# A two-layer hybrid attention and expert step: expert rows added in DRAM to the residual stream

## The reference

```
h   = rms_norm(x) * (1 + sc1) + sh1
q, k, v, gates = h @ w_in               # two attention groups, two branch gates
mixed = (sigmoid(g_a) * (o_a @ w_br_a) + sigmoid(g_b) * (o_b @ w_br_b)) @ w_out
x   = x + gt1 * mixed
h2  = rms_norm(x) * (1 + sc2) + sh2
x   = x + gt2 * moe(h2)                 # 16 experts, each token goes to 2 of them
```

## Time and profile before

| what | value |
|---|---|
| runs shown | 1655.37, 1662.59, 1666.16 us |
| median | 1662.59 us |
| span of the profiled execution | 1665.8 us |
| clock granted to TensorE, mean | 0.974 of full speed |
| PE busy | 1550.5 us, 93% of the span |
| DVE busy | 899.4 us, 54% |
| ACT busy | 700.1 us, 42% |
| POOL busy | 297.8 us, 18% |
| moved by DMA | 337.55 MB |

### The profile page before, as it was taken

The page is one execution under the profiler, slowest core; times in us unless marked ns, Lnnn a source line. Parts: engine busy times, 40 slices in busy tenths (PEclk is TensorE's granted clock), DMA queues, the critical chain, the costliest instruction groups (busy, mean ns, idle before and its releaser), DMA issues.

```text
span 1665.8 us, 21787 instructions
## 1 busy us (share of the span) xinstructions
PE 1550.5 (93%) x8180; PEld 1107.1 (66%) x8180; DVE 899.4 (54%) x1723; ACT 700.1 (42%) x1335; POOL 297.8 (18%) x321
## 2 busy tenths in 40 slices
PE   4999999999999989999779999999999999899992
PEld 1777777777787855554456777777777888555561
DVE  1566664455554752455575656543455556344554
ACT  4543554445521313444553455534454132144550
POOL 1001000011101014565200010000111010345640
PEclk9999999999999989999989999999999999999996
DMA  8541205534365379999847212353345253898847
GB/s 339 205 153 58 77 26 189 185 109 161 111 234 219 135 278 400 383 401 346 303 178 270 95 39 77 120 185 126 114 152 204 87 202 127 308 414 336 331 143 286
DMA packets 92376, 337.55 MB, mean 203 GB/s; under 512 B 20960, under 2 KB 21024, under 8 KB 89328
## 3 DMA queue, kind: packets, MB, share of 16 engines
q1 hardware_dynamic: 53136, 197.68, 32.5%
q0 software_dynamic: 38992, 135.86, 22.1%
q10 hardware_dynamic: 144, 2.62, 0.4%
HBM read 351.22 MB, written 47.35 MB: 239 GB/s over the span
## 4 chain that ended last, share of the span: by engine, by line
PE 81%; DMA 8%; DVE 6%; ACT 2%; issue 2%; SPq 1%; POOL 0%; POOLq 0%; ACTq 0%; DVEq 0%
PE ps L1884 16%; PE ps L1886 16%; PE ps L1885 16%; PE ps L2214 6%; PE ps L1876 5%; DMA gu_b<-w_gu,eidx 4%; PE ps L2263 3%; PE ps L2036 3%; PE ps L2018 2%; PE ps L1843 2%; PE ps L1792 2%; PE ps L2096 2%; PE ps L2197 2%; PE ps L2230 2%; PE ps L2070 1%
## 5 line engine op out<-in xcount | busy, mean ns | idle before, releaser
L1884 PE MATMUL ps<-hi,hT_hi 128*128 128x512 f32 x960 | 392.8, 409 | 5.5 <-ACT o_a L1094 3.0
L1886 PE MATMUL ps<-hi,hT_lo 128*128 128x512 f32 x960 | 377.1, 393 | 0.0
L1885 PE MATMUL ps<-lo,hT_hi 128*128 128x512 f32 x960 | 376.3, 392 | 0.0
L1884 PEld LDWEIGHTS ps<-hi,hT_hi 128*128 128x128 f32 x960 | 181.8, 189 | 64.8 <-issue 23.6
L1886 PEld LDWEIGHTS ps<-hi,hT_lo 128*128 128x128 f32 x960 | 181.4, 189 | 40.1
L1885 PEld LDWEIGHTS ps<-lo,hT_hi 128*128 128x128 f32 x960 | 182.2, 190 | 32.4
L890 ACT ACTIVATE hi<-raw 128x1024 fp32r<-128x1024 f32 x106 | 108.4, 1054 | 136.6 <-DMA raw<-w_stream 136.6
L1236 DVE TENSOR_TENSOR lo<-raw,hi 128x1024 fp32r<-128x1024 f32 x106 | 127.5, 1220 | 65.4 <-ACT hi L890 65.0
L1715 DVE TENSOR_TENSOR lo<-raw,hi 128x1024 fp32r<-128x1024 f32 x96 | 112.7, 1221 | 39.7 <-ACT hi L1161 33.9
L2214 PE MATMUL ps<-gu_a,xT 128*64 128x512 f32 x256 | 116.1, 607 | 6.7 <-DMA gu_b<-w_gu,eidx 6.7
L2214 PE MATMUL ps<-gu_b,xT 128*64 128x512 f32 x256 | 116.1, 607 | 0.0
(11 more groups left out here) (312 smaller groups left out, 2880.8 us busy)
## 6 DMA issues: line engine op xcount, KB each, us to landing
raw<-w_stream SPq DMA_DIRECT2D x112, 512.0 KB
raw<-w_gu SPq DMA_DIRECT2D x80, 512.0 KB
raw_m<-w_stream SPq DMA_DIRECT2D x68, 512.0 KB, 5.4
raw<-w_dn SPq DMA_DIRECT2D x40, 512.0 KB
bias_na<-na_bias POOLq DMA_DIRECT2D x32, 384.0 KB, 3.4
sg<-sg_d POOLq DMA_DIRECT2D x8, 1280.0 KB, 9.7
y<-ye_d SPq DMA_DIRECT2D x20, 512.0 KB, 5.2
raw_p<-w_stream SPq DMA_DIRECT2D x16, 512.0 KB, 16.0
```

The source lines that it names most:

```text
L1884: pe.matmul(out, w_hi, m_hi, start=first, stop=False)
L1885: pe.matmul(out, w_hi, m_lo, start=False, stop=False)
L1886: return pe.matmul(out, w_lo, m_hi, start=False, stop=last)
```

## The change

x is no longer parked and brought back. Before the expert stage it is stored to `acc[l]`, a DRAM tensor of 768 rows: 640 for the tokens and 128 spare ones; for the last layer `acc[l]` is the output itself. Each expert tile's rows, multiplied by the weight and by the token's gate vector, are added to it by an indirect DMA with `compute_op=add`. A slot without a token goes to a spare row, so each add covers all slots of its tile. A token may stand in both halves of a pair tile, so a pair tile takes two adds of 64 rows (`row_i`, `row_h`), 26 adds in a layer. Each waits until the one before has landed (`acc_done`).

DVE now makes both halves of ysb: `row_gates(n)` writes the slot's gate vector there (128x1024), and `ys(n)` multiplies it with PSUM and weight (two of 128x512). ACT's `ys` is gone. `row_gates(n-1)` stands ahead of the `hid` multiply of tile n. The gate vectors are loaded to `gtm` before the stage. After the stage, SP waits for the last add and loads x; DVE's 3 passes, the loads of the expert rows, the final stores and the second spill are gone, and the head of layer 1 works on statistics two tiles ahead. The last two tiles change places: full 8, pair 4, full 9. The descriptor area is 8192 instead of its default 16384 bytes.

```
-SCHED += [("full", j) for j in range(N_PAIR, N_FULL)] + [("pair", PAIRS[N_PAIR - 1])]
+SCHED += [("full", N_PAIR), ("pair", PAIRS[N_PAIR - 1]), ("full", N_FULL - 1)]
...
+ADDS_BEFORE = [sum(1 if full else 2 for full in IS_FULL[:n]) for n in range(MOE_TILES + 1)]
+N_ADDS = ADDS_BEFORE[MOE_TILES]
+ACC_ROWS = (NT + 1) * P
...
                 def load_back(l):
...
+                    sp.wait_ge(acc_done.sem, acc_done.at(l, N_ADDS - 1))
                     for t in range(NT):
-                        for j, dst in enumerate((Y1[t], Y2[t])):
-                            r0 = (j * NT + t) * P
-                            sp.dma_start(dst[:], ye_d[r0:r0 + P, :]).then_inc(gathered[t].sem, 16)
+                        sp.dma_start(x[:, t, :], acc_x[l][:, t, :]).then_inc(x_loaded[t].sem, 16)
...
-                        sp.dma_start(x_spill, x[:]).then_inc(x_parked.sem, 16)
+                        sp.dma_start(acc_x[l], x[:]).then_inc(x_parked.sem, 16)
...
-                if l >= 1:
-                    po.wait_ge(x_ready.sem, x_ready.at(l - 1, NT - 1))
-                    po.dma_start(x_spill, x[:]).then_inc(x_spilled.sem, 16)
...
-                def store_rows(n):
-                    po.wait_ge(y_act.sem, y_act.at(l, n))
-                    po.wait_ge(y_dve.sem, y_dve.at(l, n))
-                    po.indirect_dma_start(ye_d, bass.IndirectOffsetOnAxis(row_i[:, XD_COL[n]:XD_COL[n] + 1], 0),
-                                          ysb[n % 2][:], None, bounds_check=2 * NT * P - 1,
-                                          oob_is_err=False).then_inc(y_stored[n % 2].sem, 16)
+                def add_rows(n, h=0):
+                    a = ADDS_BEFORE[n] + h
+                    if a == 0:
+                        po.wait_ge(x_parked.sem, x_parked.at(l, 0))
+                    else:
+                        po.wait_ge(acc_done.sem, acc_done.at(l, a - 1))
+                    if h == 0:
+                        po.wait_ge(y_dve.sem, y_dve.at(l, n))
+                    p1 = P if IS_FULL[n] else HALF
+                    c = slice(XD_COL[n], XD_COL[n] + 1)
+                    rows_at = row_h[0:HALF, c] if h else row_i[0:p1, c]
+                    po.indirect_dma_start(acc[l], bass.IndirectOffsetOnAxis(rows_at, 0),
+                                          ysb[n % 2][h * HALF:h * HALF + p1, :], None, bounds_check=ACC_ROWS - 1,
+                                          oob_is_err=True, compute_op=ALU.add).then_inc(acc_done.sem, 16)
...
+                def row_gates(n):
+                    if n >= 2:
+                        dve.wait_ge(acc_done.sem, acc_done.at(l, ADDS_BEFORE[n - 1] - 1))
...
+                    return chained(STT(out=ysb[n % 2][:], in0=gtm[:, 0, :], scalar=p_slot[:, c:c + 1], in1=gtm[:, 1, :],
+                                       op0=ALU.mult, op1=ALU.add))
...
+                    if n >= 1:
+                        gated = row_gates(n - 1)
                     dve.wait_ge(silu_done.sem, silu_done.at(l, n))
                     dve.tensor_tensor(hid[:], ps[:, 0, D_EXP:2 * D_EXP], silu_g[:], ALU.mult).then_inc(hid_done.sem, 1)
...
-                else:
-                    for t in range(NT):
-                        add_rows(t, gate_rows(l, t))
```

More of the change, by code:

```diff
@@ L333, in program @@
         ysb = [in_lo("ysb0", [P, D], F32, 12), ysb1]
-        x_spill = nc.dram_tensor("x_spill", [P, NT, D], F32, kind="Internal").ap()
+        acc = [nc.dram_tensor(f"x_acc{l}", [ACC_ROWS, D], F32, kind="Internal").ap() for l in range(DEPTH - 1)] + [y_out]
+        acc_x = [a[0:NT * P, :].rearrange("(t p) d -> p t d", p=P) for a in acc]
         mod_d = nc.dram_tensor("mod_d", [DEPTH, 2, 6 * D], F32, kind="Internal").ap()
@@ L476, in program @@
         ht_lo = Signal("ht_lo", sum(IS_SPLIT))
-        y_act = Signal("y_act", MOE_TILES)
         y_dve = Signal("y_dve", MOE_TILES)
-        y_stored = [Signal(f"y_stored{b}", half[b], 0, 16) for b in range(2)]
-        gathered = [Signal(f"gathered{t}", 5 if t == 0 else 3, 0, 16) for t in range(NT)]
-        x_ready = Signal("x_ready", NT)
+        acc_done = Signal("acc_done", N_ADDS, 0, 16)
+        gtm_loaded = Signal("gtm_loaded", 2, 0, 16)
+        x_loaded = [Signal(f"x_loaded{t}", 1, 0, 16) for t in range(NT)]
         def mslot(e, s):
@@ L642, in _ @@
                 head_pair(3)
+                sp.wait_ge(mod_stored.sem, mod_stored.at(l, 3))
+                for cond in range(2):
+                    sp.dma_start(gtm[:, cond, :], mod_d[l, cond, 5 * D:6 * D].partition_broadcast(P)
+                                 ).then_inc(gtm_loaded.sem, 16)
                 def weights(j, units):
@@ L666, in _ @@
                         weights(SCHED[n - 1][1] + 2, (4, 5))
[L668 to L673, removed]
         @blk.gpsimd
@@ L1731, in ys @@
                     c = XD_COL[n]
-                    dve.tensor_scalar(ysb[n % 2][:, 512:1024], ps[:, 3, :], w_slot[:, c:c + 1], None, ALU.mult).then_inc(y_dve.sem, 1)
+                    return chained(STT(out=ysb[n % 2][:], in0=gtm[:, 0, :], scalar=p_slot[:, c:c + 1], in1=gtm[:, 1, :],
+                                       op0=ALU.mult, op1=ALU.add))
+                def ys(n, gated):
+                    dve.wait_ge(*down_done(l, n))
+                    after(gated)
+                    c = XD_COL[n]
+                    for j in range(2):
+                        half_row = ysb[n % 2][:, 512 * j:512 * j + 512]
+                        ins = STT(out=half_row, in0=ps[:, 2 + j, :], scalar=w_slot[:, c:c + 1], in1=half_row, op0=ALU.mult,
+                                  op1=ALU.mult)
+                    ins.then_inc(y_dve.sem, 1)
                 after(chained(TS(score[:], score[:], 0.5, 0.5, ALU.mult, ALU.add)))
```

140 lines of the change are left out of this document (57 added, 83 removed).

## The result

The changed kernel takes **1748.1 us** (1739.05 to 1751.1), the kernel before 1660.7 in the same session: ratio 1.0526, 95% interval 1.0488 to 1.0564, which is **+87 us**. The forecast was +20, its range ended at 1722. The sign was right and the size was not. The profiled execution has a span of 1749.2 us.

A forecast was written before the change was run, and what follows sets the result against it. PE and the DMA engines were taken as both full in the expert stages, with PE idle only at the layer and program ends. 37 + 8 + 1 - 26 = +20 us gave 1682.6 us, range 1640 to 1722.

The forecast's parts named there:

- gains at the ends: End of the program 20 us and end of layer 0 with layer 1's head 6 us: together 26 us gained.
- the adds' DMA work: Expert stages: adds over all slots, counted as two passes, 34.6 us more DMA a layer; 37 us reach PE.
- the chain of adds: Expert stages: POOL waits for each landing before the next add; 4 us a stage, 8 in all.
- the rest, and the move of the last tiles: Slot tables and gate difference cost 1 us in all; swapped last tiles only move loads, which still land before x.
- The bound of 6 us: End of the program: at 6 us an add instead of 4.0, the gain there would be 14 us.
- rival 3: Three passes or more, or the chain serializes the stage: +62, 1725 us; begins at 415 ns a packet; chance 0.23.
- Rival 2: Expert stages: the queue is full only because loads run ahead, lateness never reaches PE; 1638 us; chance 0.10.
- Rival 1: Adds cost no more than copies and the gain comes through: -16, 1647 us; chance 0.22.

The follow-up runs named there:

- the whole kernel that waits for nothing: Changed kernel with unchained plain stores to separate tensors, empty slots skipped, gate pass behind `hid`, pair's second store right behind its first: 1634.1 us, sums left out of x.
- unchained plain kernel: Changed kernel with plain indirect stores to DRAM tensors of their own in place of adds, none waiting for another: 1661.9 us, sums left out of x.
- skipped slots' plain stores: Changed kernel with unchained plain stores to tensors of their own, empty slots skipped: 1654.5 us, sums left out of x.
- chained plain kernel: Changed kernel with `compute_op=ALU.add` taken out, each store still waiting for the landing of the one before: 1702.1 us, sums left out of x.
- unchained accumulates: Changed kernel with every add after a layer's first going to a DRAM tensor of its own, none waiting for another: 1687.7 us, sums left out of x.
- the change with its two repairs: Changed kernel with gate pass behind `hid` and empty slots skipped: 1704.3 us; with the pair's second add right behind its first as well: 1717.8 us.
- the one with the gates in the stage: Kernel before, with row gates multiplied in on DVE in the expert stage, plain unchained stores, x returning in two DVE passes a tile: 1658.7 us.

## Why the prediction was wrong

The medians against before put the terms in a row, each step being one or two edits between two kernels that ran, and good to some 4 to 7 us: from -28.5 (nothing waits, plain stores) to -7.6 (second store behind the loads, gate pass ahead of `hid`), to +26.7 (accumulates over all slots), to +87.4 (the chain).

| term | forecast | measured |
|---|---|---|
| gains at the ends (measured: the whole kernel that waits for nothing) | -26 | -28.5 |
| the adds' DMA work | +37 | +34.3 |
| the chain of adds | +8 | +60.6 |
| the pair's second store behind the loads, gate pass ahead of `hid`, without chain | part of the 8 | +21.0 |
| the rest, and the move of the last tiles | +1 | not apart in these steps |
| sum | +20 | +87.4 |

The steps depend on their order: the 20 us that accumulate and chain cost only together are booked under the chain here.

**Gains at the ends: the size came, by other terms than those forecast.** In the kernel whose stores wait for nothing (1634.1 us) the ends give 34 us and the stages are 4 longer. Its end is 10.0 us (last matmul at 1624.7, span 1634.7), 20 less than before. That this is the 10 of the forecast is luck: the forecast had three chained adds, the last landing 9 us after the last matmul, and nothing behind it. There the last plain store lands 5.5 us after it, with no chain, and the drain of POOL (3.7 us) stands behind it. From the last matmul of layer 0 to layer 1's stage it is 14 us less, where 6 were forecast: the first tile's transposes in the head start 4.5 us sooner, where 1.5 later was forecast. In the changed kernel most of it is eaten again: 21.0 at the end and a gap of 23.0 us to the head, because the adds of earlier tiles are still in line when the last matmul ends. The term that failed at the ends is "For an add that also reads its row I take 4.0 us with the wait": without load an add takes 4.5 to 6.3 us and 0.7 us to the next, and the first of the last three (1727.17) stood behind another (1720.10). The bound of 6 us was near enough for an add; that the line would not be empty when the last tile came, and POOL's drain, were nowhere in the sum. The Trainium skill, "DMA: Bandwidth & Descriptors" (Anatomy of one DMA), has a sum of 2.0 us and the bytes at 436 GB/s, which makes 3.2 us for 128 rows and 2.6 for 64, estimated by that page. For a plain store of 128 rows the trace agrees (3.3 us, the last of the unchained plain kernel); it does not for plain stores of 64 (3.2 and 3.8) and for adds (6.2 for 128 rows at 897.29, 4.5 and 5.0 for 64), all without load.

**DMA work: right in engine time, and at PE right in sum but not in place.** The lines of POOL's queue on the pages of the unchained kernels, plain and then with accumulates, spans 1654.3 and 1683.8:

```profile
q0 software_dynamic: 39616, 141.62, 23.1%
```
```profile
q0 software_dynamic: 39616, 141.62, 25.7%
```

That is 382.1 and 432.7 us of all engines: an accumulate of 9.44 MB costs 25.3 us a layer more than a plain store, and one more pass at 394 GB/s had been put at 24.0. With the skipped slots' plain stores (21.7% of 1654.2 us: 359.0) the bytes are 11.6 us a layer against 10.7. Together 36.9, forecast 34.6: two passes it is. The packet records say the same for a full tile: a row of 4 KB takes 328 ns on an engine as an accumulate (median of the 128 of the last add) and 161 ns as a plain store (of the 128 of the last store in the chained plain kernel). For 64 rows they don't: 328 ns, and 307 in the plain store before the last; why stays open. The Trainium skill, "DMA: Bandwidth & Descriptors" (Rules for kernel authors), says that an accumulate reads its destination and writes it later; two passes agree with that read. At PE the forecast put all 37 us into the stages. Between the spans of the two kernels of this step (1654.2 and 1683.8 us) 24 us are in the stages and 7 at the two ends. So rival 3's condition, 415 ns a packet, wasn't met; its time was passed for its other reason, "the chain serializes the stage".

**The chain: the step that failed.** "I put 4 us a stage, 8 in all, between 0 and 10 a stage", because "this is mostly the same delay as the one just costed". It is not the same delay. The unchained accumulates do all the same DMA work and are 60.6 us faster. By spans (1683.8 and 1749.2 us) the chain takes 46 us in the stages, where PE idles more and is granted the lower clock more often, and 18 at the two ends. Three things were missed.
- *Rate.* I asked whether one add of 12 us stops PE. The question was whether 26 in a row keep up. At the median of 6.7 us and 0.7 to the next issue they need 26 x 7.4 = 192 us; in the kernel before, layer 0's stores took 186 us from the first issue (644.3) to the last landing (830.8). So even at the median the adds don't fit, and five of layer 0's take 14 to 19 us. Its 26 landings sum to 224 us and fill most of the 258 from 645.1 to 903.5; after 21 of the first 25 the next add is issued within 1.4 us. All the ingredients stood in the prediction, the 20.5 us of the earlier trace rows too; they were used for one link, never multiplied by 26. With a chain the landing sets a throughput and is no longer a latency alone.
- *Held-back loads.* The prediction named `xg`, `gu_a` and `dn` behind the wait and priced them with the rest at 4. In the kernel before, with 18 plain stores and nothing else changed, the chain costs 23 us, with PE waiting for `gu_b` 7.7 us in layer 0's stage, before 4.9 (a part of the 23 only); in the change with its two repairs and the second add at once it is 32.6 us.
- *Place in the queue.* The second add stands behind `gu_b` and two `dn`, and the gate pass that waits for it stands ahead of `hid`. The prediction saw this path ("an add that takes 12 us or more there stops PE") and did not add it as a term. Without any chain the place costs 20.7 us even with the gate pass behind `hid`, and the early pass adds nothing clear of noise; under the chain the early pass is worth 20.

**The rest.** DVE's added passes are hidden, as said. The move of the last two tiles, which the prediction let cost nothing, was +11 us in the kernel before; in the changed kernel it has no term that these runs separate. The smaller descriptor area, "nothing" too, goes with a shorter drain of POOL: 8.2 us in the three kernels with the default, 3.3 to 4.0 in all those with 8192 bytes. In the changed kernel, where nothing hides the drain, the default would cost some 4 us more, an estimate from these drains; no run changes the area alone.

**Rivals.** Rival 3 had the mechanism, the chain that serializes the stage, with a chance of 0.23. Rival 2, that lateness never reaches PE, is refuted by every chained kernel. Rival 1's sum needs adds as cheap as copies; even with copies in place of adds the chain leaves +41.

**What stays open.** How the 11 us of the swap in the kernel before divide was not tried. Nor were kernels in which PE's granted clock stays up through the waits, so its 17.5 us can't be set against the idle time. Two adds may meet at one row, so every kernel that brings the sums back into x by adds keeps the chain; what two adds in flight at one row would give wasn't tried, and the 1634.1 us are a bound of the idea, not a version. The fastest complete kernel is the one with the gates in the stage, 1658.7 us.

## What to carry to other kernels

When each DMA must wait for the one before it, count the links and multiply by the landing under load, then set that beside the stage's time; a landing that nobody waited for before says what it will be (20.5 us here), and the throughput of the queue says nothing of it. Then list what is issued behind each such wait on the same engine: an order that is best without the chain (the second store at once, -21 us) can be worse with it (+10). A read-modify-write in DRAM that saves passes at the end is paid twice over in DMA time all along the stage, which a stage with its DMA engines at 0.97 can't hide. Idle engines don't cure the chain: without load a link still takes 5 to 7 us here. And when work at the end of a program goes, look at what it hid: here the drain of POOL.

## What the hardware showed that I had not expected

- In an indirect accumulate of 128 rows of 4 KB each packet takes double the engine time of a plain store's (328 ns and 161 ns), and POOL is busy with it for a median of 1.84 us (1.46 for 64 rows), where the chained plain stores took 1.40 and 0.94. The accumulating stores of the earlier trace rows with their four rows had shown only POOL's part.
- How late an indirect DMA lands depends on what POOL queued ahead of it: the add issued at 645.06 landed after 18.7 us, behind `gu_a`, `gu_b`, two `dn` and an `xg` (5.8 MB) issued since 635 us, while the DMA engines were at 1.01 with 371 GB/s. Without load an add of 128 rows takes 6.2. Moving the pair's second plain store ahead of 3 MB of loads cut DVE's waits for it from 27.0 to 4.7 us.
- POOL ends the program with a drain: 8.2 us with the default descriptor area, 3.3 to 4.0 with 8192 bytes.
- Waits of 3 to 9 us at PE went with more than their own length: in layer 0's stage the granted clock fell from 0.98 to 0.91 in the mean, and the same 948 matmul records kept PE busy for 211.3 us in place of 199.5.
